# A gate tile and its row chain moved under other product tiles, block weights built by GpSimd, and stage barriers taken out of a two-block sequence kernel

## What is computed

```python
p = h @ w_in                      # xm (1024), z (1024), 16 gate columns
xcv = silu(dwconv1d(xm, conv) + conv_b)
q, k, v = blockdiag4(xcv, wq), blockdiag4(xcv, wk) / 16, blockdiag4(xm, wv)
logi, logf = gates_i + bi, log_sigmoid(gates_f + bf)
# per direction and head, over chunks of 128 tokens (2 of context, 4 latent):
b = cumsum(logf); m_row = running maximum of (b + m, logd)
h = (s @ v + w_inter * (C @ q)) / max(|den|, exp(-m_row))
C = carry_scale * C + v^T (k * exp(log_in - m_new))
out = ((rmsnorm(h) + c_skip * xcv) * sigmoid(z)) @ w_out
```

## Time and profile before

| | us |
|---|---|
| median of 3 runs (3350.72 to 3358.95) | 3356.83 |
| the profiled execution | 3355.57 |
| its span in the profile | 3353.8 |
| TensorE busy in it | 3068.8 |
| VectorE, ScalarE, GpSimd busy | 1875.3, 1193.8, 321.9 |

### The profile page before, as it was taken

The page is one execution under the profiler, slowest core; times in us unless marked ns, Lnnn a source line. Parts: engine busy times, 40 slices in busy tenths (PEclk is TensorE's granted clock), DMA queues, the critical chain, the costliest instruction groups (busy, mean ns, idle before and its releaser), DMA issues.

```text
span 3353.8 us, 67563 instructions
## 1 busy us (share of the span) xinstructions
PE 3068.8 (92%) x29464; PEld 2493.4 (74%) x29464; DVE 1875.3 (56%) x3016; ACT 1193.8 (36%) x2244; POOL 321.9 (10%) x196
## 2 busy tenths in 40 slices
PE   6999799978999999998797899999988999988998
PEld 4778488866888877676576688777777787868777
DVE  3134654554777741352165788436776764766854
ACT  3111444434122231233254433225344344535342
POOL 1321000002444400132000000000000000000000
PEclk9999899988999999898699899999999999999899
DMA  8651000021122222111001233232200232210222
GB/s 312 237 220 51 2 4 4 4 89 36 59 63 63 63 63 63 49 52 56 0 1 44 63 94 94 88 101 63 63 28 15 80 96 71 76 45 4 63 83 82
DMA packets 62753, 230.19 MB, mean 69 GB/s; under 512 B 7456, under 2 KB 7968, under 8 KB 62240
## 3 DMA queue, kind: packets, MB, share of 16 engines
q1 hardware_dynamic: 62496, 226.36, 20.8%
HBM read 224.24 MB, written 2.10 MB: 67 GB/s over the span
## 4 chain that ended last, share of the span: by engine, by line
PE 62%; DVE 12%; ACT 4%; issue 1%; ACTq 0%; DVEq 0%
PE bank L357 23%; PE bank L410 7%; DVE x_all L2525 4%; PE bank L2748 3%; PE bank L3314 3%; PE bank L3299 3%; PE bank L1709 2%; PE bank L1858 2%; PE bank L1857 2%; PE bank L1859 2%; PE bank L2214 2%; PE bank L1715 1%; PE bank L1714 1%; PE bank L1713 1%; DVE ring_low L1887 1%
## 5 line engine op out<-in xcount | busy, mean ns | idle before, releaser
L1829 DVE SCALAR_TENSOR_TENSOR arena<-arena,vec 128x512 f32<-128x512 f32 (+1 forms) x220 | 199.2, 922 | 25.5 <-DVE arena L1827 0.2
L2525 DVE SCALAR_TENSOR_TENSOR x_all<-arena,vec,x_all 128x512 f32<-128x512 f32 x240 | 179.9, 750 | 10.5 <-ACT arena L2635 3.7
L357 PE MATMUL bank<-h_high_ffn,w_high_ffn 128*128 128x256 f32 (+1 forms) x672 | 173.4, 340 | 4.4 <-ACT arena L1791 4.4
L1887 DVE TENSOR_TENSOR ring_low<-ring,w_high_ffn 128x1024 fp32r<-128x1024 f32 x84 | 102.5, 1223 | 133.1 <-ACT w_high_ffn L1882 129.8
L357 PE MATMUL bank<-h_low,w_high_ffn 128*128 128x256 f32 (+1 forms) x672 | 172.7, 338 | 0.0
L357 PE MATMUL bank<-h_high_ffn,ring_low 128*128 128x256 f32 (+1 forms) x672 | 171.1, 335 | 0.0
L357 PE MATMUL bank<-h_high_d,w_high_d 128*128 128x512 f32 x384 | 157.5, 410 | 5.2 <-DVE h_low_d L2687 5.2
L357 PE MATMUL bank<-h_low_d,w_high_d 128*128 128x512 f32 x384 | 153.9, 401 | 0.0
L357 PE MATMUL bank<-h_high_d,ring_low 128*128 128x512 f32 x384 | 153.7, 400 | 0.0
L1939 DVE SCALAR_TENSOR_TENSOR arena<-arena,vec 128x512 f32<-128x512 f32 x176 | 132.3, 752 | 29.3 <-ACT arena L1900 23.8
L1857 PE MATMUL bank<-h_high_ffn,w_high_ffn 128*128 128x512 f32 x352 | 140.0, 398 | 5.0 <-DVE h_low L584 5.0
(11 more groups left out here) (578 smaller groups left out, 7887.3 us busy)
## 6 DMA issues: line engine op xcount, KB each, us to landing
arena<-in_ada_w_dram SPq DMA_DIRECT2D x96, 512.0 KB, 6.1
ring<-in_ffn_up_dram SPq DMA_DIRECT2D x88, 512.0 KB, 3.5
ring<-in_d_branch_dram SPq DMA_DIRECT2D x56, 512.0 KB, 3.5
ring<-in_ffn_down_dram SPq DMA_DIRECT2D x48, 512.0 KB, 3.5
ring<-in_d_in_dram SPq DMA_DIRECT2D x32, 512.0 KB, 3.5
ring<-in_ab_in_dram SPq DMA_DIRECT2D x19, 512.0 KB, 7.3
ring<-in_c_in_dram SPq DMA_DIRECT2D x17, 512.0 KB, 3.6
ring<-in_d_join_dram SPq DMA_DIRECT2D x16, 512.0 KB, 3.5
```

The costliest lines, as they stand in the source:

```text
L357: ins = M.matmul(bank_of(tile % 2, seg), w[:, at], x(k, seg), start=first, stop=last)
L1829: ins = V.scalar_tensor_tensor(y, a, w(dy, dx), y, ALU.mult, ALU.add)
L1887: V.tensor_tensor(ring_low[slot][:, :], ring[slot][:, :], high[slot].bitcast(F32), ALU.subtract)\
L2525: ins = V.scalar_tensor_tensor(y, halves2(cpad[i][:, tap:tap + LAT]), w, y, ALU.mult, ALU.add)
```

## The change

- The gate columns of `w_in` are laid out after the xm columns, so the gate tile is tile 8, followed by eight z tiles. The z products are no longer in a loop.
- The row chain moves from `mlstm_mid_dve` into `mlstm_in_dve` (`gate_rows_dve`), right after the three-tap filter; ScalarE's steps of it are put between its z evictions: after the gate tile, after z tile 0, after z tile 5.
- `gate_columns_pe`, between z tiles 6 and 7, turns the rows: the four quantities are stacked on 128 rows of two tensors, so 12 products do it; the decays take one product with a small masked tensor (`mwide`), and their exponential follows on ScalarE after z tile 7.
- GpSimd builds the block weights (`mlstm_weights_pool`) after its 17 splits; turn n waits for the query eviction of turn n-2.
- The barriers before and after the turns go. VectorE sets the column of ones in the values (`vtk`) after the first value eviction.
- In the context units two pairs of banks take turns for the state sums; unit u waits for the state of u-2, unit 16 for both.
- First mixer: token tiles 4 and 5 are interleaved in pairs of k-steps, and each weight block counts as used after both had it; groups 8 and 9 follow the first and the last quarter. SyncE lists the first `ab_in` block between groups 8 and 9.

```diff
@@ mixer_ab_in_pe
-        for t in range(6):
-            if t >= 2:
-                pe.wait_ge(room_pe)
-            for k in range(KD):
...
+        for t in range(4):
+            if t >= 2:
+                pe.wait_ge(room_pe)
+            tokens(t, range(KD)).then_inc(prod_act.sem, 1)
             ada_part(pe, ADA_FIRST + t)
+        for k in range(0, KD, 2):
+            for t in (4, 5):
+                if k == 0:
+                    pe.wait_ge(room_pe)
+                ins = tokens(t, (k, k + 1))
+                if t == 4 and k == KD - 2:
+                    ins.then_inc(prod_act.sem, 1)
+            ins.then_inc(item_done.sem, 1)
+            if k in (0, 6):
+                ada_part(pe, ADA_FIRST + 4 + k // 6)
@@ mlstm_in_pe
-        for n, segs in ((6, BOTH), (8, LATENT), (1, BOTH)):
+        for n, segs in ((7, BOTH), (7, LATENT)):
             split_product_pe(pe, n, wh_m, part(hh_m), part(hlT), segs)
+        gate_columns_pe(pe)
+        split_product_pe(pe, 1, wh_m, part(hh_m), part(hlT), LATENT)
+
+    def gate_columns_pe(pe):
+        pe.wait_ge(made_act)
+        for c in range(NC6):
+            for i, r in enumerate((RA, RX)):
+                dst = psum[6][:, 32 * c + 16 * i:32 * c + 16 * i + 16].rearrange("p (d h) -> p d h", d=4)
+                ins = M.matmul(dst, r[:, P * c:P * c + P], head_rows(ident), start=True, stop=True)
+        ins.then_inc(prod.sem, 1)
+        M.matmul(psum[7][:, 0:48], ones[0:64, :], mwide[0:64, :], start=True, stop=True).then_inc(prod_act.sem, 1)
@@ mlstm_in_act
         tiles_act(act, 1, gates)
+        act.wait_ge(to_act)
+        link(act, act_step, S.activation(RW[r, :], RX[r, :], ACT.Abs))
+        S.activation(RW[r, :], RW[r, :], ACT.Exp, scale=-1.0).then_inc(to_dve.sem, 1)
+        z_tiles(0, 1)
+        act.wait_ge(to_act)
+        S.activation(RW[r, :], RW[r, :], ACT.Ln).then_inc(to_dve.sem, 1)
+        z_tiles(1, 6)
+        act.wait_ge(to_act)
+        S.activation(RA[64:128, :], RW[r, :], ACT.Exp, scale=-1.0)
+        S.activation(RX[r, :], RX[r, :], ACT.Exp, scale=-1.0)
+        S.activation(RX[64:128, :], RK[r, :], ACT.Exp).then_inc(made_act.sem, 1)
+        z_tiles(6, 8)
+        act.wait_ge(prod_act)
+        S.activation(csb.rearrange("p u c -> p (u c)"), psum[7][:, 0:48], ACT.Exp, scale=-1.0)
@@ block weights
+    def mlstm_weights_pool(pool):
+        loaded(pool, 9)
+        for n in range(KD):
+            if n >= 2:
+                pool.e.wait_ge(tile_read.sem, block_starts["qkv"] + 3 * n - 1)
             for a in range(3):
-                ins = V.tensor_tensor(bdm[n % 2][:, P * a:P * a + P].rearrange("p (g o) -> p g o", o=4),
+                ins = G.tensor_tensor(bdm[n % 2][:, P * a:P * a + P].rearrange("p (g o) -> p g o", o=4),
                                       bdw[:, a, n, :].unsqueeze(1).to_broadcast([P, 32, 4]),
                                       diag4.rearrange("p (g o) -> p g o", o=4), ALU.mult)
@@ mlstm_scan_pe
+    k_banks = [banks[:, at:at + 1024].rearrange("p (a v) -> p a v", a=2) for at in (1024, 2048)]
+    def k_sums(u):
+        return k_banks[u % 2 if u < CONTEXT_UNITS else 0]
...
+            if u == CONTEXT_UNITS:
+                pe.wait_ge(state_taken, 2)
...
-                if u:
+                if u >= 2 and u != CONTEXT_UNITS:
                     pe.wait_ge(state_taken)
@@ SyncE
-        ada_sp(sp, ADA_FIRST + 1, ADA_TILES)
-        weights_sp(sp, A["ab_in"], 2)
+        ada_sp(sp, ADA_FIRST + 1, ADA_TILES - 1)
+        weights_sp(sp, A["ab_in"], 1)
+        ada_sp(sp, ADA_TILES - 1, ADA_TILES)
+        weights_sp(sp, A["ab_in"], 2, start=1)
@@ TensorE (the same on ScalarE and VectorE; two fewer on GpSimd and SyncE)
         mlstm_in_pe(pe)
-        phase(pe)
         mlstm_mid_pe(pe)
-        phase(pe)
         mlstm_scan_pe(pe)
```

More of the change, by code:

```diff
@@ L802, in mixer_ab_in_pe, with tokens @@
             landed[(pe.items + j) % SLOTS].skip(pe, 16)
-        for t in range(6):
-            if t >= 2:
-                pe.wait_ge(room_pe)
-            for k in range(KD):
+        def tokens(t, ks):
+            for k in ks:
                 slot = (pe.items + k // 2) % SLOTS
@@ L1971, in build @@
     mrow = mroom.take(24)
+    mwide = mroom.take(48)
     dens = [mroom.take(4), mroom.take(4)]
@@ L2047, in mlstm_in_dve @@
                 .then_inc(to_act.sem, 1)
[L2048 to L2109, removed]
@@ L2174, in mlstm_mid_dve, with mlstm_mid_pe @@
-        V.tensor_copy(ctk.rearrange("p c q d h -> p (c q d h)"), psum[6][:, 0:192])
-        V.tensor_copy(csb.rearrange("p u c -> p (u c)"), psum[7][:, 0:48])
+    def mlstm_mid_pe(pe):
+        block_starts["qkv"] = tile_read.seen["pe"]
+        for n in range(KD):
+            pe.wait_ge(weights_made)
+            w = bdm[n % 2]
+            for src, m in ((xmT, 2), (xcT, 1)):
+                pe.wait_ge(tile_read)
+                for c in range(NC6):
+                    p = pe.tiles % 2
+                    dst = psum[2 * p + 1][:, P * c:P * c + P] if c < 2 else psum[2 * p][:, P * (c - 2):P * (c - 1)]
+                    ins = M.matmul(dst, src[:, n, P * c:P * c + P], w[:, P * m:P * m + P], start=True, stop=True)
+                ins.then_inc(prod_act.sem, 1)
+                pe.tiles += 1
+            pe.wait_ge(tile_read)
+            p = pe.tiles % 2
+            for m in range(2):
+                ins = M.matmul(psum[2 * p + m][:, :], w[:, P * m:P * m + P], xcT[:, n, CTX:T], start=True, stop=True)
+            ins.then_inc(prod_act.sem, 1)
+            pe.tiles += 1
@@ new lines, in mlstm_mid_act @@
+    def mlstm_mid_act(act):
+        for n in range(KD):
+            for what, scale in (("v", 1.0), ("k", C_SCALE)):
+                act.wait_ge(prod_act)
+                p, at = act.tiles % 2, slice(P * (n % 2), P * (n % 2) + P)
+                dst = vtk[:, :, n // 2, at] if what == "v" else ktk[:, :, P * n:P * n + P]
+                S.activation(dst[:, 0:2], psum[2 * p + 1][:, 0:256].rearrange("p (c f) -> p c f", c=2),
+                             ACT.Identity, scale=scale)
+                S.activation(dst[:, 2:6], psum[2 * p][:, :].rearrange("p (c f) -> p c f", c=4),
+                             ACT.Identity, scale=scale).then_inc(tile_read.sem, 1)
+                act.tiles += 1
+            act.wait_ge(prod_act)
+            p = act.tiles % 2
+            S.activation(qstage(n), psum[2 * p][:, :], ACT.Identity)
+            S.activation(kqT[:, n, :], psum[2 * p + 1][:, :], ACT.Identity, scale=C_SCALE).then_inc(tile_read.sem, 1)
+            act.tiles += 1
@@ L2284, in take_state @@
             dve.wait_ge(prod)
-            sums, decay, n = K_SUMS[:, :, 0:VONE], csb[:, m, c:c + 1], nvec[:, 2 * h:2 * h + 2]
+            sums, decay, n = k_sums(u)[:, :, 0:VONE], csb[:, m, c:c + 1], nvec[:, 2 * h:2 * h + 2]
             if i == 0 and d == 0:
@@ L3413, in _ @@
             weights_sp(sp, A[f"d_in{l}"], 2)
-            for _ in range(1 if l else 5):
+            for _ in range(1 if l else 3):
                 phase(sp)
```

64 lines of the change are left out of this document (33 added, 31 removed).

## The result

The changed kernel takes 3304.63 us (median of 4 runs, 3303.09 to 3305.39), the kernel before beside it 3357.89; the ratio is 0.9845, 95% interval 0.9828 to 0.9862. The profiled executions have spans of 3302.5 and 3353.8 us, 51.3 less. The forecast was 3286, in a range of 3276 to 3305: the direction and nearly all mechanisms held, and the time is 18.6 us above the forecast, just inside the range. It is also the time of the rival "the change does not cover the chain" (3306), which had a chance of 0.06.

The account below looks back on a forecast made before the run. TensorE, busy 92% of the span, was taken as the bound, with time in its waits and low clock. 3355.57 less 36.5, 27.2 and 6.7 gives 3285.2; the median 1.3 above gives 3286, range 3276 to 3305.

Parts of the forecast that it names:

- the change does not cover the chain: Rival: VectorE at half speed beside GpSimd's splits, some 20 us coming out at the gate columns; 3306, chance 0.06.
- The scans take 17.1 us, to 1538.5: Row chain under the z tiles: VectorE's scans start at 1521.4 and take 17.1 us.
- nothing is late, with 1.2 us to spare on ScalarE and 3.5 on VectorE: Row chain: exponentials done at 1548.5, before TensorE wants them at 1549.7; VectorE's tail done at 1542.5.
- the 1 us that was set aside for the clock: Gate columns and last z tile: 1 us taken for low clock, between nothing and 2 us lost.
- the term of 36.5: Second mixer, input tiles to scan: the scan starts at 1597.3 instead of 1633.86, 36.5 us less.
- two rivals that did not come true: Low clock in the context units, chance 0.12, and GpSimd setting the turns' pace, 0.08; each 3299.
- another page's rule, on the ratio of speeds: Block weights: two-input elementwise work belongs on VectorE, as GpSimd takes about twice as long.
- The turns without barriers and GpSimd's weights: Before the scan: eight turns at 4.50 us; GpSimd multiplications of 0.57 us each, up to 1.07 costing nothing.
- the term of 27.2: Scan's context units: two bank pairs at full clock take 20.3 us instead of 47.5, 27.2 less.
- The rival of a low clock: Context units: waits bring clock 0.50 back, the part takes some 33 us instead of 20.3; 3299, chance 0.12.
- the first mixer's term: First mixer: first tile starts at 97.2 instead of 102.02 and a cold start goes, 6.7 us less.

Follow-up runs that it names:

- x1: The changed kernel with GpSimd splitting only 8 of the 1024 columns of each of the eight z blocks; 3288.95 us.
- x5: The kernel before with only the two pairs of banks for the state sums in the context units added; 3332.38 us.
- x4: The kernel before with only the first mixer's interleaved token tiles and SyncE's new order added; 3350.96 us.
- x2: The changed kernel with the gate columns after the last z tile instead of before it; 3290.03 us.
- x3: The changed kernel with one pair of banks for all state sums instead of two; 3324.16 us.
- x8: x2 with four buffers instead of two for the scaled keys of the context units; 3286.86 us.
- x6: The changed kernel with GpSimd rounding the high part of the z splits in full, the low part on 8 columns only; 3290.18 us.

## Why the prediction came out as it did

**The row chain** is the step that failed: "The scans take 17.1 us, to 1538.5", and with it "nothing is late, with 1.2 us to spare on ScalarE and 3.5 on VectorE". The 17.1 came from rows of a stretch in which GpSimd did nothing; under the z tiles it splits a block per tile, and a duration isn't carried along when the neighbour changes. The chain took 27.9 (x1: 17.5 without the splits). The tail took 3.9 us, as counted, and ScalarE's exponentials ended at 1553.54 instead of 1548.5.

What TensorE lost by it: the wait, 6.04; the columns 5.82 instead of 3.1, at the low clock, 2.7; the last z tile 7.38 instead of 5.56, 1.8; between turns and scan 2.2 instead of 1.9, 0.3. Less the 1 us that was set aside for the clock this is 9.8, and the term of 36.5 measured 26.9 (1633.86 less 1604.98, less the 2.0 by which everything came earlier there). The rival at 3306 had the right place, but "half speed" was the wrong mechanism and its price of 20 us twice the real one; its time is the measured one only because gain is missing elsewhere too, which is luck. Its 0.06 rested on the 3.5 us to spare. That the time lies inside the range is luck as well: the top was built from two rivals that did not come true, and the chain was placed outside. As it is worded, half of what is between 3299 and 3306, the top would be 3302.5 and not 3305, and the measured time outside.

The trace of before could have told it. A stretch in front of the second mixer has GpSimd's first splits beside VectorE's small operations on the modulation; the timelines of GpSimd and of VectorE there, before:

```profile
1415.75 2.35 POOL L328 TENSOR_TENSOR ring_low<-ring,w_high_m 128x1024 fp32r<-128x1024 f32 x1
1418.06 1.06 POOL L327 TENSOR_SCALAR w_high_m<-ring 128x1024 fp32r<-128x1024 f32 x1
```

```profile
1415.68 0.16 DVE L741 TENSOR_TENSOR modv<-mods,vec 128x16 f32<-128x16 f32 x1
1415.77 2.35 DVE L739 SCALAR_TENSOR_TENSOR modv<-mods,vec 128x16 f32<-128x16 f32 x1
...
1418.12 1.02 DVE L741 TENSOR_TENSOR modv<-mods,vec 128x16 f32<-128x16 f32 x1
```

The addition of line 741, on sixteen columns, takes 0.16 us at 1415.68, just before GpSimd's operation of 1415.75 begins, and 1.02 at 1418.12, when GpSimd's next one began at 1418.06. Between them an operation on sixteen columns takes 2.35, as long as the GpSimd operation that began just before it. Even a row that the prediction quotes has it: GpSimd's first rounding in the first mixer takes 1.84 instead of 1.05, while VectorE is in a long two-input operation. The rule is in the Trainium skill, SBUF — State Buffer, section SBUF: two separate sides: GpSimd shares one pair of ports with VectorE's operations that have two inputs in SBUF or run in a two-port mode, and whichever starts first keeps it for its whole instruction. The trace agrees: 2.35 beside 2.35 here, and an end at 1538.31 beside one at 1538.30 above. The prediction weighed another page's rule, on the ratio of speeds, which changed nothing.

**The turns without barriers and GpSimd's weights** were right. Turns of 4.50 us, no wait for weights; one multiplication costs 0.46 us (1.38 a turn), forecast 0.57, inside the 3.2 us that are free.

**The context units**: 21.96 us against the 20.3 forecast, the mechanism and the high clock as described; the term of 27.2 measured 25.6. A round of two takes 2.47 to 2.53 instead of 2.4. The rival of a low clock (0.12) fell, and x5 shows that it would have fallen with a cold start too.

**The first mixer**: the first tile starts at 96.50, forecast 97.2, and what follows comes 7.2 us earlier, forecast 6.7. Of these only 2.0 are left when the second mixer's xm tiles are evicted. The same code then ran at another clock in places; the stretch after and before, columns as in the earlier trace rows:

```profile
358.00:369.00 11.00, 7.98 (x12) 2.87 (x10) 7.48 (x12) 0.00 (x0) 0.00 (x0) 0.52 0.00 0
```

```profile
365.00:376.00 11.00, 6.40 (x14) 2.95 (x15) 9.23 (x13) 0.00 (x0) 0.00 (x0) 0.83 0.00 0
```

It isn't a cost of the change as such: x4, with this part alone, still has 6.1 us when those tiles are evicted and 5.0 at the end, and x2, with the same code up to the last z tile, is 4.4 us ahead of the changed kernel when its row chain begins. Which stages run at which level there differs between kernels with the same code, and why is open; no run was made on it.

The sum: 26.9 + 25.6 + 2.0, less 3.2 given back after the context units (54.5 ahead there, 51.3 at the end), is 51.3, where 70.4 had been forecast. Half of the 19.1 us between them is the chain, 9.6; the context units are 1.6. The other 7.9 are gain that was given back in stretches that the change doesn't touch: 4.7 of the first mixer's term, and the 3.2 after the context units. These 3.2 aren't lost each time either: x2 is 68.0 us ahead of the kernel before at that place and 67.3 at the end.

## What to carry to other kernels

Before a chain of VectorE operations moves beside GpSimd's work, add to its length the GpSimd instructions that it will meet, whole ones: a small operation pays as much as a large one. That is an upper bound, since some operations are not held and one that began first runs to its end; here seven instructions of 12.8 us in all cost the chain 10.3. Look for a place in the trace of before where both engines work at once, and read single instructions there, not means. And where TensorE waits for an eviction after every short burst, a second pair of banks can be worth more than the wait itself: here it decided at which clock the products ran.

## What was not expected of the hardware

- VectorE and GpSimd hold each other up, in both directions. In the changed kernel a GpSimd operation and a two-input VectorE operation of 3072 columns both begin at 95.47; the latter takes its 3.36 us, the former 5.62 instead of 2.39.
- Not all of VectorE is held: a copy of 32x1 inside a GpSimd operation took its 0.14 us (at 1536.14 above), while the one-input operation of 64x768 at 1515.21 took 1.42 instead of 0.55.
- Units of 1.1 us of products and 0.9 us of waiting lose the high clock after the third (x3); with two pairs of banks TensorE has no wait at the low clock, and has the high one back after three units (x5); after that its 0.36 us of waiting per two units don't lose it.
- Behind twenty-four records of products of 16 columns and two of 48 the clock fell in x2 and stayed at 1.00 in x8, where both kernels run the same code; before the last z tile it fell in x6 and stayed in x1.
